# RWKV-7 and pool encoder: head norm refined in three parts, and four steps of the head stage moved in their queues

## The reference

```python
def wkv_step(S, inp):
    r_t, w_t, k_t, v_t, a_t, b_t = inp
    sa = jnp.einsum('bhvk,bhk->bhv', S, a_t)
    S = S * w_t[:, :, None, :] + sa[..., None] * b_t[:, :, None, :] + v_t[..., None] * k_t[:, :, None, :]
    y = jnp.einsum('bhvk,bhk->bhv', S, r_t)
    return S, y
...
    ys = layer_norm(ys, lnx_g.reshape(N_HEADS, HEAD_DIM), lnx_b.reshape(N_HEADS, HEAD_DIM), LNX_EPS)
    ys = ys + jnp.sum(rh * kh * r_k.astype(jnp.float32), axis=-1, keepdims=True) * vh
    out = ys.reshape(B, T, D_RWKV).astype(zr.dtype) * g
```

## Time and profile before

| what | value |
|---|---|
| median of 3 runs | 2667.56 us (2666.09 to 2676.43) |
| the profiled execution | 2670.87 us, span 2669.1 us |
| TensorE busy | 2538.0 us (95%), 27280 matmuls |
| VectorE busy | 1694.4 us (63%) |
| ScalarE busy | 932.8 us (35%) |
| GpSimd busy | 1580.7 us (59%) |
| mean granted clock of TensorE | 0.986 of 2.4 GHz |

### The profile page before, as it was taken

The page is one execution under the profiler, slowest core; times in us unless marked ns, Lnnn a source line. Parts: engine busy times, 40 slices in busy tenths (PEclk is TensorE's granted clock), DMA queues, the critical chain, the costliest instruction groups (busy, mean ns, idle before and its releaser), DMA issues. The chain is left out here.

```text
span 2669.1 us, 65842 instructions
## 1 busy us (share of the span) xinstructions
PE 2538.0 (95%) x27280; PEld 2446.9 (92%) x27280; DVE 1694.4 (63%) x2492; ACT 932.8 (35%) x1942; POOL 1580.7 (59%) x1303
## 2 busy tenths in 40 slices
PE   7999999989998999999999999999899889999997
PEld 7999999977777999999999999988777789999996
DVE  6866418756665789931598981477566558898124
ACT  3444104444432245410245530144455214554002
POOL 5555666734324667666767766656334256776664
PEclk9999999989999999999999999999999999999998
DMA  4232332200001232223323323321000012232222
GB/s 153 89 103 80 93 100 78 74 2 5 4 13 42 85 105 96 95 82 96 87 94 104 103 77 89 99 79 49 4 4 5 27 57 95 96 103 84 87 87 77
DMA packets 81899, 193.65 MB, mean 73 GB/s; under 512 B 13681, under 2 KB 14065, under 8 KB 81649
## 3 DMA queue, kind: packets, MB, share of 16 engines
q1 hardware_dynamic: 78192, 187.07, 21.8%
q10 hardware_dynamic: 3456, 3.02, 0.3%
HBM read 186.95 MB, written 3.12 MB: 71 GB/s over the span
## 5 line engine op out<-in xcount | busy, mean ns | idle before, releaser
L852 PE MATMUL ps<-xa,w_hi 128*128 128x272 f32 x2208 | 583.4, 289 | 4.0 <-DVE w_lo L1759 2.4
L852 PE MATMUL ps<-xa,w_lo 128*128 128x272 f32 x1932 | 560.5, 290 | 0.0
L852 PE MATMUL ps<-xb,w_hi 128*128 128x272 f32 x1656 | 478.9, 289 | 0.0
L644 POOL TENSOR_SCALAR w_hi<-w_raw 128x1024 fp32r<-128x1024 f32 (+2 forms) x225 | 236.8, 1052 | 394.0 <-PE ps L738 386.9
L852 PEld LDWEIGHTS ps<-xa,w_hi 128*128 128x128 f32 x2208 | 399.2, 189 | 6.5 <-DVE w_lo L1759 3.2
L648 POOL TENSOR_TENSOR w_lo<-w_raw,w_hi 128x640 fp32r<-128x640 f32 (+2 forms) x225 | 366.5, 1629 | 0.0
L852 PEld LDWEIGHTS ps<-xa,w_lo 128*128 128x128 f32 x1932 | 364.1, 188 | 0.0
L852 PEld LDWEIGHTS ps<-xb,w_hi 128*128 128x128 f32 x1656 | 312.6, 189 | 0.0
L738 PE MATMUL ps<-hh,w_hi 128*128 128x272 f32 x1472 | 305.0, 288 | 5.6 <-DVE hl L1787 5.4
L738 PE MATMUL ps<-hh,w_lo 128*128 128x272 f32 x1472 | 302.7, 288 | 0.0
L738 PE MATMUL ps<-hl,w_hi 128*128 128x272 f32 x1472 | 302.3, 287 | 0.0
(11 more groups left out here) (353 smaller groups left out, 5683.3 us busy)
## 6 DMA issues: line engine op xcount, KB each, us to landing
w_raw<-in_wz SPq DMA_DIRECT2D x44, 512.0 KB, 3.3
w_odd<-in_w1i SPq DMA_DIRECT2D x72, 256.0 KB, 2.9
w_odd<-in_w2i SPq DMA_DIRECT2D x72, 256.0 KB, 2.9
w_raw<-in_w1i SPq DMA_DIRECT2D x68, 256.0 KB, 2.8
w_raw<-in_w2i SPq DMA_DIRECT2D x64, 256.0 KB, 2.8
w_raw<-in_w1o SPq DMA_DIRECT2D x32, 448.0 KB, 3.3
w_raw<-in_w2o SPq DMA_DIRECT2D x32, 448.0 KB, 3.3
w_raw<-in_w2i SPq DMA_DIRECT2D x20, 512.0 KB, 3.2
```

What stands on the lines that cost most here:

```text
L644: pool.tensor_scalar(w_hi[k][:, 0:nk, :], w_raw[k][:, 0:nk, :], 1.0, 0.0, ALU.mult, ALU.add).then_inc(w_hi_done, 1)
L852: mm = pe.matmul(ps[:, bank(site, b, j), 0:HT], w, x, start=(j in FRESH and k + i == 0), stop=(k == 3 and i == 2), skip_group_check=True)
```

## The change

No instruction is added or removed. In half_b on VectorE the three Newton instructions are spread: the first ahead of H1's eviction, the second behind the state of chunk 0, the third behind H2's eviction (new function refine; newton stays for pair 5 and the layer norms). TensorE and VectorE work chunk 0 ahead of H2 instead of behind it. ScalarE's gain and bias go from slot 5 to slot 6, and each carry of half_b to the end of the slot before. In half_a ScalarE's y_tile(2) goes ahead of the carry of slot 6, and sample_state behind the carry of slot 7. At the seam of two halves, VectorE's piece 9 (a) stays in slot 8 and piece 8 (r) goes to slot 9, behind X3's eviction; TensorE's token_major(0) waits for a alone and products for r too. For the first pair of a layer the pieces stay as they were.

```diff
-        IN_B = {0: (0, 1), 3: (6,), 8: (8, 9)}
+        IN_B = {0: (0, 1), 3: (6,), 8: (9,), 9: (8,)}
...
                 pe.wait_ge(tm_ready, due)
+                pe.wait_ge(ar_ready, n * 3 + 3)
...
-                        used = [(ar_ready, n * 3 + 3), (bk_ready, n * 3 + 3), (vc_ready, n + 1)]
+                        used = [(ar_ready, n * 3 + (2 if right else 3)), (bk_ready, n * 3 + 3), (vc_ready, n + 1)]
...
                     elif k == 2:
                         products(1, n)
-                    else:
+                    elif k != 5:
                         step(k - 3, 1, n)
...
                         chunk_y(k - 5, l, p)
+                    if k == 5:
+                        step(k - 3, 1, n)
...
-                if k == 5:
+                if k == (6 if p < NPAIR - 1 else 5):
                     act.wait_ge(pt_ready, n + 1)
...
+                    if right and k == 6:
+                        y_tile(2, l, p - 1)
                     if right and 4 <= k < 8:
                         carry(k, l, p - 1)
-                    if right and k == 6:
+                    if right and k == 7:
                         sample_state(l, p - 1)
...
-                    if right and k in (6, 8, 9):
-                        y_tile({6: 2, 8: 3, 9: 4}[k], l, p - 1)
+                    if right and k in (8, 9):
+                        y_tile({8: 3, 9: 4}[k], l, p - 1)
...
-                    if 6 <= k < 9:
-                        carry(k - 5, l, p)
...
                         prepare_2(l, p + 1, q, False)
+                    if 5 <= k < 8:
+                        carry(k - 4, l, p)
...
-                    dve.wait_ge(ar_ready, n * 3 + 2)
+                    dve.wait_ge(ar_ready, n * 3 + (2 if first else 1))
...
+            def refine(l, p, i):
+
+                n = l * NPAIR + p
+                r, tmp = prs[:, :], psq[:, :]
+                if i == 0:
+                    dve.wait_ge(prs_ready, n + 1)
+                    dve.scalar_tensor_tensor(halves(tmp), pair_bank(5), LNX_EPS, halves(r), ALU.add, ALU.mult).then_inc(hn_newton, 1)
+                    return
+                dve.wait_ge(hn_newton, n * 3 + i)
+                if i == 1:
+                    dve.scalar_tensor_tensor(tmp, tmp, -0.5, r, ALU.mult, ALU.mult).then_inc(hn_newton, 1)
+                else:
+                    dve.scalar_tensor_tensor(r, tmp, 1.5, r, ALU.add, ALU.mult).then_inc(hn_newton, 1)
...
+                    if norm_before and k == 4:
+                        refine(l, p - 1, 0)
-                    if k >= 3:
+                    if k >= 3 and k != 5:
                         step(k - 3, 1, n)
                     if 5 <= k < 9:
                         chunk_out(k - 5, l, p)
+                    if norm_before and k == 5:
+                        refine(l, p - 1, 1)
+                    if k == 5:
+                        step(k - 3, 1, n)
+                    if norm_before and k == 5:
+                        refine(l, p - 1, 2)
```

More of the change, by code:

```diff
@@ L2044, in normalise @@
                     dve.tensor_tensor(halves(pd[:, :]), halves(row(zs, p)), pair_bank(5), ALU.subtract).then_inc(pd_ready, 1)
+                if p < NPAIR - 1:
+                    return
                 if k == 4:
@@ L2047, in normalise @@
                     newton(head_norm(p)[1][:, :], psq[:, :], pair_bank(5), LNX_EPS, hn_newton, n * 3)
-                if p < NPAIR - 1:
-                    return
-                if k == 4:
                     dve.wait_ge(hn_newton, n * 3 + 3)
```

## The result

The changed kernel takes 2657.47 us (median of 16 runs, 2649.29 to 2668.71), the kernel before 2668.36 us in as many runs beside it (2659.28 to 2679.63). The ratio is 0.9948, with a 95% interval from 0.9934 to 0.9962: 13.9 us less (10.1 to 17.6). The ratio isn't that of the two medians, which are 10.9 apart. The forecast was 2652 us with a range of 2645 to 2661, and the 0.5% line that the prediction drew lies inside the interval of the ratio. The profiled execution took 2650.34 us, 20.5 less than the one of before.

The account below looks back on a forecast made before the run. Waits hopping between engines in the two head stages bound the kernel, about 4 us per pair. Terms 8.7 + 0.7 + 5.0 + 0.6 + 0.0 = 15.0 us gave 2652.6, with 0.6 for the clock 2652 us, range 2645 to 2661.

Parts of the forecast that it names:

- the 0.5% line: Whole kernel: 2654.2 us, 13.3 us less, about what a measurement can tell from no change; chance of faster 0.56.
- Newton step and chunk 0: half_b, slots 4 to 6: state of chunk 1 comes 0.87 us earlier, x 10 = 8.7 us.
- The bounds' lower end: half_b, Newton step and chunk 0: 0.16 us if only ScalarE's lateness goes; the upper bound was 1.15.
- The y eviction: half_a, slots 5 to 7: TensorE's state_y no longer waits for y; 0.63 us x 8 = 5.0 us.
- the last two half_a of a layer: y eviction with no table load there: 0.15 us each, x 4 = 0.6 us (0 to 0.63 each).
- The seam: Slots 8, 9, 0: r behind X3's eviction would win 0.19 us, taken back by a's stretching and keys waiting for r.
- sum of the seam 0.0: Slots 8, 9, 0: net effect 0.0 us per seam, from -0.2 to +0.19, for 10 seams.
- The sum of the walk: All places: 8.7 + 0.7 + 5.0 + 0.6 + 0.0 = 15.0 us saved.
- The low clock: half_a slots where TensorE waits for y: one low stretch may stay at full clock, counted as 0.6 us gain.
- the partial case: Rival: steps in slots 4 to 6 slip, 0.4 in place of 0.87, sum 9.3 us, 2658 us; chance 0.22.
- the given-back case: Rival: first Newton instruction before H1's eviction, or keys behind r, becomes the chain; 2665 to 2668 us; chance 0.08.
- The rival by the clock: Slower rival: new low-clock stretches in 15 halves (5 half_a, 10 half_b) cost 21.9 us, 2674 us; chance 0.04.

Follow-up runs that it names:

- e4: Kernel before with only ScalarE's half_b changed: gain and bias in slot 6, carries at the end of the slot before; 2668.43 us, one execution.
- e1: Kernel before with only half_a's ScalarE order changed: y_tile(2) ahead of the carry, sample_state behind the next; 2655.25 us, ratio 0.9953.
- e9: Kernel before with two more sample-state copies on ScalarE ahead of the y eviction; full pair 46.00 us, four of eight with a short low stretch.
- e5: Kernel before with Newton step split, gain in slot 6, carries earlier, but TensorE's chunk 0 still behind H2; 2680.22 us, one execution.

## Why the prediction was right

**Newton step and chunk 0: right in place, short by little.** It said 0.87 us; the state of chunk 1 comes 0.82 earlier. The steps hold one by one: H1's eviction isn't held (1.49 us after prs begins, as in the earlier trace rows); G16's eviction 3.97 us behind H1's, walked 3.95; the gain 5.02 behind, walked 5.09; the first pair's interval -0.99 with y's 0.61 in it, so 0.38 for chunk 0 where I took 0.35. The bounds' lower end, 0.16, is what moving the gain alone gives at that state (0.15 in e4), and it does not even reach the period: e4 is 0.23 slower.

**The y eviction: right.** 0.63 expected, 0.62 measured, with and without the rest. In the last two half_a of a layer it gave 0.32 and 0.25, where I took 0.15 each. L2018 takes 0.98 us in place of 1.77 in the kernels with y early, so no loss came of it, as weighed.

**The seam: right in sum, wrong as a part by itself.** All its steps came as told: a 1.17 us (1.2 told), ending 0.59 after GpSimd's instruction, kkb as r ends, and a wait for tm worth 0.16 (0.1 told). But "sum of the seam 0.0" holds only against a kernel whose GpSimd norm has not moved. The norm's later GpSimd instruction would have stretched r in the old order and cost 0.35 to 0.4 of the 0.82; the seam takes r out of its way. Alone the parts give 0.44, 0.62 and -0.01, together 1.41: the missing 0.36 belongs to both. The prediction walked the combined queue, so its sum held while its split into parts did not. The section of the Trainium skill that it weighed, "Who interferes with whom" in "SBUF — State Buffer", is borne out by every one of these: 1.08 to 1.17 us where GpSimd's instruction is still running, 0.71 or 0.72 where it has ended.

**The sum of the walk.** 15.0 was told. Measured per layer: 0.99 + 3 x 1.41 + 1.29 + 1.05 = 7.6, twice 15.1. That it agrees to 0.1 us is in part luck: over both layers the first place with the seam gave 0.4 us less than told, the last half_a's 0.5 more.

**The low clock: the term that was mis-sized.** I counted 0.6 us of gain. The short stretches went altogether, 3 x 1.45 = 4.4 us in the profile of before, and the rows with y early show why: they come behind TensorE's wait for y. Walk and short stretches make 19.5 us, but the runs show 13.9, so 5 to 6 us are given back. The runs show where: in the clock, not in the walk. At a mean clock of 0.986 three runs of the changed kernel take 2650.3 to 2653.7 us, and four of the kernel before beside e1 2665.9 to 2671.0: at the same clock the walk's 15 us are there in full. But the changed kernel's clock is lower, 0.979 to 0.988 in its 16 runs (median 0.984), against 0.982 to 0.990 (median 0.986) in the 19 of the kernel before beside e1, although the short stretches are gone. With y alone it is 0.986 to 0.993 (median 0.992), with the norm alone 0.985 to 0.989. So the edits don't add up in time as they do in the pair periods: 12.5 us with y alone and 8.0 with the norm alone, 13.9 with all, though the intervals are wide (6 to 19 and 2 to 14).

Which low stretches grow more frequent is open. The long ends are one candidate, at 7.9 to 8.1 us each: in the traces they are 5 of 8 with y and norm both changed, and 5 of 18 otherwise (with a sixth, shorter one in e9, 41.44 us), too few to tell apart. The low stretches outside pairs and stage ends are another: they add up to 41 to 65 us in the 14 profiles. A mean clock can't tell the two: the filled kernel's profile has 0.988 with no long end, the first one of the changed kernel 0.986 with one.

The rivals: the partial case (first place 0.4) is what VectorE's order gives without TensorE's (0.42 in e5); the given-back case had the wrong mechanism (H1's eviction isn't held, and the wait behind keys is worth 0.16 us), but something was given back, by the clock. The rival by the clock looked for it in the wrong place: half_b stayed at full clock and the full pairs lost their low stretches, while the clock over the whole run fell.

## What to carry to other kernels

Walk the queues with all parts of a change in place: an edit that is worth nothing alone (the seam) can be what lets another keep its gain, and a part of another (the gain's move) can cost time alone. A wait of 0.7 us on TensorE in a repeated place can be worth more than its length: here the clock fell behind it in 20 of 64 pairs. Count low stretches over several executions before and after, and compare runs at equal mean clock: that separates what the walk wins from what the clock gives or takes. At the end of a stage with short dependent steps look at the windows behind it: here 12 us in which TensorE was busy for 2.3 to 2.5 of every 4 us were followed by 20 us at half clock in some executions.

## What the runs showed of the hardware

- Low stretches of 3.4 us appear in half_a in 20 of 64 pairs where TensorE waits 0.7 to 1.0 us for y, 0.8 to 1.6 us after that wait, and in none of 48 where it doesn't wait. They cost 1.45 us each; which pair has one changes from execution to execution.
- The stretch at 0.50 at a stage's end lasts 20.5 us and costs 7.9 to 8.1 us. It comes in some executions of one kernel and not in others (none and one in the two profiles of the kernel before), so with two ends it can make up to 16 of the 20 us between runs of one kernel. With filler of 1.18 us of TensorE time in each of five slots it was not seen, in one profile.
- A VectorE instruction of 128x544 with two SBUF inputs that starts while a GpSimd instruction of 1.34 us runs ends 0.57 to 0.59 us after that one's end, whatever the overlap: a takes 1.17 us (80.18 for 79.59 in the changed kernel), r 1.08 to 1.12, L2018 1.77 or 0.98.
